# Two-batch head loads, value product before the maxima, and the first head's maxima beside the last query norm in a one-core decoder trunk

## The chip, the cores and the metric

The kernel runs on one core of a Trainium2 chip. The metric is the device time of one launch in microseconds. TensorE (PE) multiplies, ScalarE (ACT) and VectorE (DVE) work on its results, GpSimd (POOL) fills constants, SyncE (SP) issues nearly all DMAs; each engine runs its own instructions strictly in order and waits on semaphores for the others.

## The reference

One step of a two-layer decoder trunk over a prompt of 1,024 tokens with 16 meta tokens in front (1,040 rows) and a decode batch of 8 sequences of 4 tokens: layer 0 is a gated short convolution and an MLP, then one shared K/V/log-forget side is computed, layer 1 is forget-gated attention and an MLP. What matters here is the prompt's attention:

```
def forget_attention(q, k, v, c_q, c_k, q_pos, k_pos):
    s = einsum('nqhd,nkhd->nhqk', q, k) * HEAD_DIM ** -0.5
    s = s + (c_q[..., :, None] - c_k[..., None, :])     # c = cumsum of log f
    s = where(k_pos <= q_pos, s, -1e30)
    p = softmax(s, axis=-1)
    return einsum('nhqk,nkhd->nqhd', p, v)
```

There are 16 heads of 64 dimensions. q and k are RMS-normed per head. All is float32.

## The kernel before, in words

Float32 accuracy comes from splitting each operand into a rounded part (hi, float32r) and a rest (lo); a product is hi x hi + lo x hi + hi x lo. The rounding runs on ACT, the subtraction on DVE.

**Projections.** Weights come in units of 128 columns; `unit` (L415) multiplies one, 72 matmuls. The query units U_Q..U_Q+7 end the projection phase. For each, DVE scales the result into `KW` (L1667), ACT squares it, PE sums the squares per head (`column_sums`, L469), ACT takes the root, DVE finishes the norm into `QS` (`head_fin`, L1805), ACT and DVE split it into `STH`/`STL` (`stage_hi` L1548, `stage_lo` L1812) and SP stores both to DRAM (`stage_out`, L1361 and L1363). Keys were staged so before.

**Head operands.** `load_head(h)` fetches from DRAM what head h needs, into one of two halves (even and odd heads): six transfers of 260 KB (L929: `QA` = q hi, `CK` = k hi, `QB` = q lo and q hi, `DK` = k hi and k lo), the two rows of cumulated forget values (L930), and a zero row (L931), all on one semaphore. The tile names in the trace are q_hi_ext (QA), k_hi_ext (CK), q_lo_hi (QB), k_hi_lo (DK). SP's order in step h is: `spread_sums(h-1)` (L939), `load_inverse(h-1)` (L946, L949: store 1/sums, wait, fetch it broadcast), `load_v` at even h (L918, L919), `load_head(h+2)` once all logits of head h are done, `load_logf`.

**Maxima.** A head's row maxima come before its logits. `max_logits(h, u)` has 18 uses: 15 write hi x hi logits (L578, mask L581) to one of two PSUM banks in turn (4 and 5), DVE reduces each (L596); three ("A", "B", "C", L572) turn the maxima into a row that ACT copies into QA (`keep_shift`, L617). A use waits until the one two before it has been read. The maxima need QA and CK alone; QB and DK are first read by `logits`.

**The loop.** A head has 8 groups. PE's step t does `logits(t+2)` (L635, L636, L639), the maxima of head h+1 listed for this group, `weigh_values(t)` (L712 to L714). ACT takes two exponentials of each group (L658, L663), DVE the difference (`probs_lo`, L675), and then reduces the step's maxima; in group 4 it inverts the sums of head h-1 (L731) and in group 7 divides (L738). `max_logits(h+2, 0)` stands in step 8(h+1) and waits for the whole of `load_head(h+2)`.

**The start.** `attention_loads` loads head 0 after the stores of query block 6 (stage 14), `attention_vector` clears the value tiles on DVE, and POOL makes the mask (L1030) and, when stages 14 and 15 are stored, clears the odd half's tiles (`extend(1)`, from L1015) and `NMR` (L1038). The odd half's QA and CK lie where STH0/STL0 (even stages) were, QB and DK where STH1/STL1 were. DVE and PE start the maxima of head 0 after these.

## Time and profile before

| what | us |
|---|---|
| three runs, median (lowest to highest) | 3050.04 (3049.43 to 3050.2) |
| the profiled execution, its own time | 3054.29 |
| its span, first to last instruction | 3052.5 |
| PE busy | 2814.7 (92%) |
| DVE busy | 1189.4 (39%) |
| ACT busy | 792.0 (26%) |
| mean granted TensorE clock | 0.959 |

The shares are of the whole span. The prompt's attention takes about 1540 to 2017 us of it; in that stretch PE is busy in 6 to 8 tenths, elsewhere in 9. The profile's chain of work that ended last gives PE 85% and DMAs 4% of the span.

### The profile page before, as it was taken

How to read it: one execution, taken by the hardware profiler on the slowest of the kernel's cores; microseconds unless marked ns; L12 is line 12 of the kernel's file. 1: busy time of each engine (PE TensorE's matmuls, PEld its weight loads, DVE VectorE, ACT ScalarE, POOL GpSimd, SP SyncE). 2: the span in 40 equal slices, each digit the busy share in tenths (PEclk: the TensorE clock that was granted, in tenths of full speed). 3: DMA queues.
4: the chain of work that ended last, by engine and by line, in shares of the span. 5: the costliest groups of instructions: out<-in, count | busy, mean ns of one | idle time of the engine just before them, and what ended most of it. 6: DMA issues, size and time to landing. Idle time of an engine off the chain costs nothing.

```text
span 3052.5 us, 41584 instructions
## 1 busy us (share of the span) xinstructions
PE 2814.7 (92%) x17026; PEld 2729.9 (89%) x17026; DVE 1189.4 (39%) x1343; ACT 792.0 (26%) x1127; POOL 96.6 (3%) x65
## 2 busy tenths in 40 slices
PE   6999999999999999999967677767899999999999
PEld 5999999999999999999957666655799999999999
DVE  4444344133242333343455455554335223142331
ACT  4111121011110123532544444444322111011111
POOL 3000010000000002000000000000020000000000
PEclk8999999999999999999978888879899999999999
DMA  3111111111111111442343332323011111111112
GB/s 94 50 41 48 42 42 48 42 49 42 42 47 41 49 42 35 141 127 74 104 127 75 91 80 66 82 82 130 22 41 42 49 42 49 41 48 41 43 48 71
DMA packets 256005, 188.52 MB, mean 62 GB/s; under 512 B 15088, under 2 KB 237232, under 8 KB 255906
## 3 DMA queue, kind: packets, MB, share of 16 engines
q1 hardware_dynamic: 236802, 178.14, 20.6%
q10 hardware_dynamic: 19104, 8.99, 1.0%
q8 instruction: 71, 1.16, 0.2%
q14 instruction: 28, 0.23, 0.0%
HBM read 156.47 MB, written 30.49 MB: 61 GB/s over the span
## 4 chain that ended last, share of the span: by engine, by line
PE 85%; DMA 4%; DVE 3%; ACT 2%; SPq 2%; issue 1%; POOL 1%; ACTq 0%; DVEq 0%; POOLq 0%
PE ps L415 74%; DMA q_hi_ext<-k_hi_ext 3%; PE ps L578 2%; SPq L929 2%; PE ps L875 1%; PE ps L798 1%; DVE max_parts L596 1%; PE ps L712 1%; PE ps L713 1%; PE ps L714 1%; POOL t L450 1%; PE ps L635 1%; PE ps L469 1%; PE ps L636 1%; DMA inv_rows<-inv_spread 0%
## 5 line engine op out<-in xcount | busy, mean ns | idle before, releaser
L400 DVE TENSOR_TENSOR w_lo<-w_raw,w_hi 128x1024 fp32r<-128x1024 f32 x192 | 235.1, 1224 | 1234.5 <-ACT w_hi L392 1234.5
L415 PE MATMUL ps<-x_hi,w_hi 128*128 128x358 f32 x2688 | 594.6, 329 | 16.9 <-DVE x_lo L443 16.7
L415 PE MATMUL ps<-x_hi,w_lo 128*128 128x358 f32 x2688 | 591.0, 328 | 0.0
L415 PE MATMUL ps<-x_lo,w_hi 128*128 128x358 f32 x2688 | 589.9, 328 | 0.0
L392 ACT ACTIVATE w_hi<-w_raw 128x1024 fp32r<-128x1024 f32 x192 | 203.4, 1060 | 1324.4 <-PE ps L415 1324.4
L415 PEld LDWEIGHTS ps<-x_hi,w_hi 128*128 128x128 f32 x2688 | 465.7, 190 | 20.7 <-DVE x_lo L443 10.4
L415 PEld LDWEIGHTS ps<-x_lo,w_hi 128*128 128x128 f32 x2688 | 467.4, 190 | 0.0
L415 PEld LDWEIGHTS ps<-x_hi,w_lo 128*128 128x128 f32 x2688 | 466.4, 190 | 0.0
L415 PE MATMUL ps<-hid_hi,w_hi 128*128 128x358 f32 x1920 | 423.4, 329 | 3.1 <-DVE hid_lo L1215 3.1
L415 PE MATMUL ps<-hid_hi,w_lo 128*128 128x358 f32 x1920 | 420.8, 327 | 0.0
L415 PE MATMUL ps<-hid_lo,w_hi 128*128 128x358 f32 x1920 | 420.0, 327 | 0.0
L415 PEld LDWEIGHTS ps<-hid_hi,w_hi 128*128 128x128 f32 x1920 | 332.7, 190 | 3.3 <-issue 3.3
L415 PEld LDWEIGHTS ps<-hid_hi,w_lo 128*128 128x128 f32 x1920 | 332.5, 189 | 0.0
L415 PEld LDWEIGHTS ps<-hid_lo,w_hi 128*128 128x128 f32 x1920 | 331.8, 189 | 0.0
L578 PE MATMUL ps<-k_hi_ext,q_hi_ext 128*128 128x512 f32 (+5 forms) x240 | 101.0, 442 | 127.2 <-DMA q_hi_ext<-k_hi_ext 99.8
L578 PEld LDWEIGHTS ps<-k_hi_ext,q_hi_ext 128*128 128x128 f32 (+1 forms) x240 | 48.0, 204 | 149.4 <-DMA q_hi_ext<-k_hi_ext 93.2
L1454 ACT ACTIVATE hid_hi<-t 128x1074 f32 (+1 forms) x72 | 79.4, 1102 | 291.1 <-DVE t L1757 260.2
L1671 DVE TENSOR_TENSOR hid_lo<-t,hid_hi 128x1074 f32 (+1 forms) x72 | 92.0, 1278 | 100.1 <-ACT hid_hi L1454 100.1
L596 DVE TENSOR_REDUCE max_parts<-ps 128x1 f32<-128x512 f32 (+5 forms) x176 | 96.4, 564 | 43.0 <-PE ps L578 25.0
L450 POOL TENSOR_TENSOR t<-t,t 128x1074 f32<-128x1074 f32 x25 | 70.3, 2811 | 1275.4 <-ACT t L434 1274.9
L1731 DVE TENSOR_TENSOR acc<-ps,acc 128x1074 f32 (+1 forms) x80 | 101.5, 1269 | 22.4 <-PE ps L415 22.4
L675 DVE TENSOR_TENSOR probs_lo<-probs_f,probs_hi 128x768 fp32r<-128x768 f32 (+3 forms) x128 | 97.6, 762 | 26.9 <-ACT probs_hi L663 25.5
(228 smaller groups left out, 2514.7 us busy)
## 6 DMA issues: line engine op xcount, KB each, us to landing
w_raw<-in_mlp_w SPq DMA_DIRECT2D x128, 512.0 KB, 3.8
w_raw<-in_conv_w_in SPq DMA_DIRECT2D x24, 512.0 KB, 3.6
w_raw<-in_w_kv SPq DMA_DIRECT2D x16, 512.0 KB, 4.7
k_page<-in_cache_k SPq DMA_DIRECT2D x16, 512.0 KB, 4.1
v_page<-in_cache_v SPq DMA_DIRECT2D x16, 512.0 KB, 3.8
kh_rows<-staged_hi SPq DMA_DIRECT2D x8, 520.0 KB, 2.6
kl_rows<-staged_lo SPq DMA_DIRECT2D x8, 520.0 KB, 3.1
qh_rows<-staged_hi SPq DMA_DIRECT2D x8, 520.0 KB, 2.6
```

The source lines that it names most:

```text
L392: act.activation(WH[:, s], RAW[:, s], ACT.Copy).then_inc(w_hi, 1)
L400: dve.tensor_tensor(WL[:, s], RAW[:, s], WH[:, s].bitcast(F32), ALU.subtract).then_inc(w_lo, 1)
L415: mm = pe.matmul(PS[:, G * s + g, 0:GW], w[:, s, k], x[:, k, g * GW:(g + 1) * GW], start=(k == 0 and n == 0), stop=(k == KC - 1 and n == 2))
L450: pool.tensor_tensor(T2[:, 0:T], T2[:, 0:T], squares(f, m), ALU.add).then_inc(x_ssq, 1)
L469: mm = pe.matmul(PS[:, b, 0:GW], weights[:, :], x[:, g * GW:(g + 1) * GW], start=not stop, stop=stop)
L578: mm = pe.matmul(PS[0:rows, bank, 0:b - a], QA[hh][:, P * i:P * i + rows], CK[hh][:, a:b], start=True, stop=not diagonal)
L596: dve.tensor_reduce(to, PS[0:rows, bank, 0:b - a], mybir.AxisListType.X, ALU.max).then_inc(red_done, 1)
L675: dve.tensor_tensor(PBL[:, t % HI_RING, 0:nb * w], PF[:, t % 2, 0:nb * w], PBH[:, t % HI_RING, 0:nb * w].bitcast(F32), ALU.subtract).then_ ...
L929: sp.dma_start(to.bitcast(F32), src[rows]).then_inc(h_loaded[hh], 16)
L1454: act.activation(HH[:, j], T1[:, :], ACT.Copy).then_inc(hid_hi, 1)
L1671: dve.tensor_tensor(HL[:, j], T1[:, :], HH[:, j].bitcast(F32), ALU.subtract).then_inc(hid_lo, 1)
L1731: dve.tensor_tensor(banks(ACC[:, m]), result(c), banks(ACC[:, m]), ALU.add).then_inc(unit_read, 1)
```

## The change

`load_head` keeps the four transfers that the maxima need (QA, CK, the forget rows, the zero row); the other four become `load_cross`, on a semaphore of its own (`x_loaded`), for which `logits` waits at a head's first group. In the loop SP issues `load_head(h+2)`, `load_v`, `load_cross(h+2)` in this order. PE's step t does `logits(t+2)`, `weigh_values(t)`, then the maxima. At the start, head 0 is loaded after stage 12 and ahead of the two w_o units; POOL makes the mask as soon as the last projection unit is done, ACT rounds it before stage 14's rounding; PE does uses 0 to 4 of head 0, then the norm sums of the last query block, then the rest; DVE does uses 0 to 7, `head_fin` of the last block and some clears, uses 8 to 10, `stage_lo` of the last block, and the rest; POOL does the larger clears; head 1 is loaded in two parts, after stages 14 and 15.

```diff
-        MASKF, _ = place("mask_f32", [P, P], offset=early[0])
+        MASKF, _ = place("mask_f32", [P, P], offset=prompt_end[0])
@@ -560,7 +561,7 @@
             _, hh = head(h)
             x, bank, _ = use_of(h, u)
             if u == 0:
-                pe.wait_ge(h_loaded[hh], 128 * (h // 2 + 1))
+                pe.wait_ge(h_loaded[hh], 64 * (h // 2 + 1))
             ring_wait(h, u)
             if isinstance(x, str):
                 if x == "A":
@@ -626,6 +627,8 @@
             if h == HEADS:
                 return
             _, hh = head(h)
+            if g == 0:
+                pe.wait_ge(x_loaded[hh], 64 * (h // 2 + 1))
             if g == 0 or CHUNK_OF[g] != CHUNK_OF[g - 1]:
                 pe.wait_ge(nm_kept, N_SH * h + CHUNK_OF[g] + 1)
@@ -924,11 +927,19 @@
                 own, other = halves(hh)
                 o, rows = other.start, slice(HD * h, HD * h + HD)
                 ge(sp, st_done, NG * (h - 1))
-                for to, src in ((QA[hh][own], qh_rows), (CK[hh][own], kh_rows), (QB[hh][own], ql_rows),
-                                (QB[hh][other], qh_rows), (DK[hh][own], kh_rows), (DK[hh][other], kl_rows)):
+                for to, src in ((QA[hh][own], qh_rows), (CK[hh][own], kh_rows)):
                     sp.dma_start(to.bitcast(F32), src[rows]).then_inc(h_loaded[hh], 16)
                 sp.dma_start(CK[hh][o + 1:o + 3].bitcast(F32), c_rows[h]).then_inc(h_loaded[hh], 16)
                 sp.dma_start(QA[hh][o:o + 1].bitcast(F32), CK[hh][o + 3:o + 4].bitcast(F32)).then_inc(h_loaded[hh], 16)
+
+            def load_cross(h):
+
+                _, hh = head(h)
+                own, other = halves(hh)
+                rows = slice(HD * h, HD * h + HD)
+                for to, src in ((QB[hh][own], ql_rows), (QB[hh][other], qh_rows),
+                                (DK[hh][own], kh_rows), (DK[hh][other], kl_rows)):
+                    sp.dma_start(to.bitcast(F32), src[rows]).then_inc(x_loaded[hh], 16)
             def spread_sums(h):
@@ -950,17 +961,23 @@
             sp.wait_ge(c_stored, 32)
             sp.wait_ge(ext_ready, 4)
+            sp.wait_ge(st_kept[0], 32 * (KC // 2 + 1))
             load_head(0)
-            stage_out(2 * KC - 1)
+            load_cross(0)
+            for c in range(2):
+                load_unit(a["w_o"][0], 0, P * c, U_O + c)
+                stage_out(2 * KC - 3 + c)
             sp.wait_ge(unit_done, U_O)
-            sp.wait_ge(z_fin, 2 * KC)
+            sp.wait_ge(unit_read, U_O)
             sp.wait_ge(kv_stored, 48 * 2 * KC)
-            sp.wait_ge(vo_ones, 9)
+            sp.wait_ge(v_zero, 1)
             load_v(0)
             sp.wait_ge(st_kept[0], 32 * KC)
+            sp.wait_ge(ext_ready, 8)
+            load_head(1)
+            stage_out(2 * KC - 1)
             sp.wait_ge(st_kept[1], 32 * KC)
-            sp.wait_ge(ext_ready, 9)
-            load_head(1)
+            load_cross(1)
             sp.wait_ge(ids_loaded, 16)
             def load_pages(cache, to, index, done):
@@ -983,10 +1000,12 @@
                 if h:
                     spread_sums(h - 1)
                     load_inverse(h - 1)
+                if h + 2 < HEADS:
+                    load_head(h + 2)
                 if h % 2 == 0 and h + 2 < HEADS:
                     load_v(h // 2 + 1)
                 if h + 2 < HEADS:
-                    load_head(h + 2)
+                    load_cross(h + 2)
                 load_logf(h)
                 if h in (2, 4):
                     load_k(0, h // 2 - 1)
@@ -1026,16 +1045,18 @@
             pool.wait_ge(x_ssq, 24)
             extend(0)
             pool.wait_ge(unit_done, U_O)
-            pool.wait_ge(z_fin, 2 * KC)
             pool.memset(MASKF[:, :], 0.0).then_inc(p_const, 1)
             pool.wait_ge(p_const, 1)
             pool.affine_select(out=MASKF[:, :], in_=MASKF[:, :], compare_op=ALU.is_ge, fill=MASKED, base=0,
                                pattern=[[-1, P]], channel_multiplier=1).then_inc(p_const, 1)
             pool.wait_ge(p_const, 2)
             pool.wait_ge(st_kept[0], 32 * KC)
-            pool.wait_ge(st_kept[1], 32 * KC)
             extend(1)
-            pool.memset(NMR[:, :, :].bitcast(F32), 0.0).then_inc(ext_ready, 1)
+            for hh in range(2):
+                _, other = halves(hh)
+                pool.memset(VL[:, hh, :, other].bitcast(F32), 0.0).then_inc(vo_ones, 1)
+                pool.memset(VH[:, hh, 0:NT - 1, other].bitcast(F32), 1.0).then_inc(vo_ones, 1)
+                pool.wait_ge(vo_ones, 2 * hh + 2)
@@ -1066,15 +1087,10 @@
                 mask_of(i)
         def attention_scalar():
-            act.wait_ge(unit_done, U_O)
-            act.wait_ge(z_fin, 2 * KC)
-            act.wait_ge(p_const, 2)
-            act.activation(MASK[:, :], MASKF[:, :], ACT.Copy).then_inc(p_round, 1)
-            act.activation(IDR[:, :], ident[:, :], ACT.Copy).then_inc(p_round, 1)
-            act.activation(NID[:, :], ident[:, :], ACT.Copy, scale=-1.0).then_inc(p_round, 1)
+            keep_shift(0, "A")
             values_hi(0)
-            for x in "ABC":
-                keep_shift(0, x)
+            keep_shift(0, "B")
+            keep_shift(0, "C")
             for t in range(NG * HEADS):
                 exp_logits(t)
@@ -1129,22 +1145,7 @@
             for m in range(KC):
                 act.activation(HH[:, m], QS[:, m], ACT.Copy).then_inc(o_hi, 1)
-        def attention_vector():
-            dve.wait_ge(unit_done, U_O)
-            dve.wait_ge(z_fin, 2 * KC)
-            dve.memset(VRAW[:, NT - 1], 0.0).then_inc(vo_ones, 1)
-            for hh in range(2):
...
-            dve.memset(P8H[:, :, :].bitcast(F32), 0.0).then_inc(vo_ones, 1)
-            dve.memset(P8L[:, :, :].bitcast(F32), 0.0).then_inc(vo_ones, 1)
-            dve.wait_ge(vo_ones, 9)
-            for hh in range(2):
-                _, other = halves(hh)
-                dve.memset(VH[0:LASTP, hh, NT - 1, other].bitcast(F32), 1.0).then_inc(vo_ones, 1)
-            dve.wait_ge(ext_ready, 9)
+        def attention_vector(head_fin, stage_lo):
             def max_turn(h, u):
@@ -1155,8 +1156,26 @@
                         if n == REDS_FOR[x]:
                             join_max(h, x)
+            dve.wait_ge(unit_done, U_O)
+            dve.memset(VRAW[:, NT - 1], 0.0).then_inc(v_zero, 1)
+            dve.memset(NMR[:, :, :].bitcast(F32), 0.0).then_inc(v_zero, 1)
+            dve.wait_ge(v_zero, 2)
             for u in range(NUSE):
                 max_turn(0, u)
+                if u == 7:
+                    head_fin(2 * KC - 1, 1, G_QN, QS[:, KC - 1])
+                    for hh in range(2):
+                        _, other = halves(hh)
+                        dve.memset(VH[:, hh, NT - 1, other].bitcast(F32), 0.0).then_inc(v_zero, 1)
+                    dve.memset(P8H[:, :, :].bitcast(F32), 0.0).then_inc(v_zero, 1)
+                    dve.memset(P8L[:, :, :].bitcast(F32), 0.0).then_inc(v_zero, 1)
+                    dve.wait_ge(v_zero, 6)
+                    for hh in range(2):
+                        _, other = halves(hh)
+                        dve.memset(VH[0:LASTP, hh, NT - 1, other].bitcast(F32), 1.0).then_inc(v_zero, 1)
+                if u == 10:
+                    stage_lo(2 * KC - 1, QS[:, KC - 1, 0:NPR])
+            dve.wait_ge(vo_ones, 4)
             values_lo(0)
             probs_lo(0)
             for t in range(NG * HEADS):
@@ -1214,20 +1233,25 @@
                 dve.wait_ge(o_hi, m + 1)
                 dve.tensor_tensor(HL[:, m], QS[:, m], HH[:, m].bitcast(F32), ALU.subtract).then_inc(o_lo, 1)
-        def attention_tensor():
+        def attention_tensor(norm_sums):
             pe.wait_ge(p_round, 3)
-            pe.wait_ge(vo_ones, 11)
+            pe.wait_ge(unit_read, U_O)
             for u in range(NUSE):
                 max_logits(0, u)
+                if u == 4:
+                    for f in norm_sums.values():
+                        f()
             logits(0)
             logits(1)
+            pe.wait_ge(aux_read, AX_Q + 3 * KC)
+            pe.wait_ge(v_zero, 8)
             for t in range(NG * HEADS):
                 h, g = divmod(t, NG)
                 logits(t + 2)
+                weigh_values(t)
                 if h + 1 < HEADS:
                     for u in USE_AT[g]:
                         max_logits(h + 1, u)
-                weigh_values(t)
@@ -1389,9 +1413,6 @@
                 load_unit(a["w_q"][0], 0, P * n, U_Q + n)
                 if n >= 3:
                     stage_out(KC + n - 3)
-            for c in range(2):
-                load_unit(a["w_o"][0], 0, P * c, U_O + c)
-                stage_out(2 * KC - 3 + c)
             attention_loads(stage_out)
             with sp.Fori(1, KC // 2) as i:
                 for c in range(2):
@@ -1631,6 +1652,11 @@
             round_unit(U_Q + 2)
             for n in range(KC):
                 head_squares(U_Q, n)
+                if n == KC - 1:
+                    act.wait_ge(p_const, 2)
+                    act.activation(MASK[:, :], MASKF[:, :], ACT.Copy).then_inc(p_round, 1)
+                    act.activation(IDR[:, :], ident[:, :], ACT.Copy).then_inc(p_round, 1)
+                    act.activation(NID[:, :], ident[:, :], ACT.Copy, scale=-1.0).then_inc(p_round, 1)
                 if n:
                     stage_hi(KC + n - 1, QS[:, n - 1, 0:NPR])
                     round_unit(U_Q + n + 2)
@@ -1890,10 +1916,7 @@
                 if n:
                     stage_lo(KC + n - 1, QS[:, n - 1, 0:NPR])
                     cut_unit(U_Q + n + 2)
-            head_fin(2 * KC - 1, 1, G_QN, QS[:, KC - 1])
-            stage_lo(2 * KC - 1, QS[:, KC - 1, 0:NPR])
-
-            attention_vector()
+            attention_vector(head_fin, stage_lo)
             residual_turns(U_O, 4)
@@ -2036,10 +2059,7 @@
             with pe.Fori(1, KC // 2) as i:
                 unit(U_Q, i, mid=head_sums(U_Q, 1, ax(AX_Q - 3, 6, i), KC + 2 * i - 1))
                 unit(U_Q + 1, i, mid=head_sums(U_Q, 0, ax(AX_Q, 6, i), KC + 2 * i))
-            for f in head_sums(U_Q, 1, ax(AX_Q + 3 * (KC - 1), 0, 0), 2 * KC - 1).values():
-                f()
-
-            attention_tensor()
+            attention_tensor(head_sums(U_Q, 1, ax(AX_Q + 3 * (KC - 1), 0, 0), 2 * KC - 1))
             eight(U_O, 0, HH, HL, o_ready)
             mlp(1, 4, 3)
```

## Rows read from the trace of the kernel before

**Rows 1.** PE's waits, 1595 to 2005 us: total us, times, longest
```profile
PE ps L578 <- DMA q_hi_ext<-k_hi_ext: 90.3, 14, 9.0
PE ps L578 <- DVE max_parts L596: 12.1, 14, 0.9
```
**Rows 2.** Stretches: us, busy us (instructions) of PE, PEld, DVE, ACT, POOL, PEclk, DMA share, GB/s
```profile
1602.00:1976.50 374.50, 270.36 (x1716) 247.46 (x1716) 204.42 (x377) 166.57 (x325) 0.00 (x0) 0.86 0.35 81
...
1619.00:1623.00 4.00, 4.00 (x35) 3.91 (x33) 2.12 (x6) 2.40 (x6) 0.00 (x0) 1.00 0.83 206
1623.00:1628.00 5.00, 1.07 (x7) 0.87 (x7) 2.16 (x3) 2.63 (x5) 0.00 (x0) 0.97 1.00 212
1743.90:1747.70 3.80, 0.00 (x0) 0.00 (x0) 0.00 (x0) 0.00 (x0) 0.00 (x0) 0.50 0.62 130
1747.70:1754.00 6.30, 6.27 (x24) 6.03 (x25) 2.34 (x5) 1.90 (x4) 0.00 (x0) 0.50 0.00 0
1754.00:1770.00 16.00, 14.65 (x108) 13.29 (x107) 11.63 (x24) 8.98 (x20) 0.00 (x0) 1.00 0.17 44
```
**Rows 3.** Timeline, head loads of 1602 to 1630: start, us, engine, line, [idle <- releaser]
```profile
1602.11 0.47 PE L578 MATMUL ps<-k_hi_ext,q_hi_ext 128*128 128x128 f32 x1 [3.79 <-DMA q_hi_ext<-k_hi_ext]
1616.84 0.24 DVE L731 RECIPROCAL inv_spread<-sums_spread 65x16 f32<-65x16 f32 x1
1618.44 0.51 SPq L949 DMA_DIRECT2D inv_sums<-inv_rows  x1
1619.00 0.59 SPq L929 DMA_DIRECT2D q_hi_ext<-qh_rows  x1
1623.31 0.55 SPq L931 DMA_DIRECT2D q_hi_ext<-k_hi_ext  x1
1629.21 0.48 PE L578 MATMUL ps<-k_hi_ext,q_hi_ext 128*128 128x128 f32 x1 [5.14 <-DMA q_hi_ext<-k_hi_ext]
```
**Rows 4.** Timeline of one head's cycle, 1736 to 1764
```profile
1736.61 0.50 SPq L949 DMA_DIRECT2D inv_sums<-inv_rows  x1
1740.17 1.23 DVE L738 TENSOR_TENSOR q_all<-o_and_sums,inv_sums 64x1040 f32<-64x1040 f32 x1 [0.74 <-DMA inv_sums<-inv_rows]
1747.73 0.48 PE L578 MATMUL ps<-k_hi_ext,q_hi_ext 128*128 128x128 f32 x1 [7.38 <-DMA q_hi_ext<-k_hi_ext]
1749.40 0.63 PE L712 MATMUL ps<-probs_hi,v_hi 128*128 128x384 f32 x1
1751.64 0.52 PE L635 MATMUL ps<-q_hi_ext,k_hi_ext 128*128 128x256 f32 x1
1763.00 0.25 DVE L731 RECIPROCAL inv_spread<-sums_spread 65x16 f32<-65x16 f32 x1
```
**Rows 5.** Timeline, PE at full clock: one value product between two logits groups
```profile
1993.54 0.28 PE L712 MATMUL ps<-probs_hi,v_hi 128*128 128x272 f32 x1
1994.29 0.34 PE L635 MATMUL ps<-q_hi_ext,k_hi_ext 128*128 128x384 f32 x1
```
**Rows 6.** Timeline of the first head's start, 1537 to 1573
```profile
1540.87 1.05 ACT L1548 ACTIVATE staged_hi<-q_all 128x1040 fp32r<-128x1040 f32 x1
1542.40 0.67 PE L469 MATMUL ps<-squares_r,ones_per_head 128*128 128x358 f32 x1 [5.13 <-DVE squares_r L1799]
1543.41 1.22 DVE L400 TENSOR_TENSOR w_lo<-w_raw,w_hi 128x1024 fp32r<-128x1024 f32 x1
1546.75 1.34 DVE L1805 SCALAR_TENSOR_TENSOR q_all<-k_work,vectors,t 128x1074 f32<-128x1074 f32 x1 [2.12 <-ACT t L1557]
1554.48 0.44 PE L578 MATMUL ps<-k_hi_ext,q_hi_ext 128*128 128x128 f32 x1 [9.49 <-DMA q_hi_ext<-k_hi_ext]
1556.57 0.96 POOL L1015 MEMSET k_hi_ext<- 64x1040 f32 x1 [7.69 <-DMA ql_rows<-staged_lo]
1561.13 0.69 PE L578 MATMUL ps<-k_hi_ext,q_hi_ext 128*128 128x384 f32 x1 [5.56 <-DVE row_max L596]
1572.66 0.67 PE L635 MATMUL ps<-q_hi_ext,k_hi_ext 128*128 128x384 f32 x1
```

More of the change, by code:

```diff
@@ L327, in trunk @@
         p_const, p_round, ext_ready = sem("p_const"), sem("p_round"), sem("ext_ready")
-        h_loaded, sm_loaded, inv_stored, inv_loaded = (
-            [sem(f"{x}{i}") for i in range(2)] for x in ("h_loaded", "sm_loaded", "inv_stored", "inv_loaded"))
+        h_loaded, x_loaded, sm_loaded, inv_stored, inv_loaded = (
+            [sem(f"{x}{i}") for i in range(2)]
+            for x in ("h_loaded", "x_loaded", "sm_loaded", "inv_stored", "inv_loaded"))
         v_loaded, v_hi, v_lo = sem("v_loaded"), sem("v_hi"), sem("v_lo")
@@ L333, in trunk @@
         pv_done, acc_free = sem("pv_done"), sem("acc_free")
-        vo_ones, inv_done, o_fin = sem("vo_ones"), sem("inv_done"), sem("o_fin")
+        v_zero, vo_ones, inv_done, o_fin = sem("v_zero"), sem("vo_ones"), sem("inv_done"), sem("o_fin")
         ids_loaded, lp_loaded, vn_loaded = sem("ids_loaded"), sem("lp_loaded"), sem("vn_loaded")
@@ L1130, in attention_scalar @@
                 act.activation(HH[:, m], QS[:, m], ACT.Copy).then_inc(o_hi, 1)
-        def attention_vector():
-            dve.wait_ge(unit_done, U_O)
-            dve.wait_ge(z_fin, 2 * KC)
-            dve.memset(VRAW[:, NT - 1], 0.0).then_inc(vo_ones, 1)
-            for hh in range(2):
-                _, other = halves(hh)
-                dve.memset(VH[:, hh, 0:NT - 1, other].bitcast(F32), 1.0).then_inc(vo_ones, 1)
-                dve.memset(VH[:, hh, NT - 1].bitcast(F32), 0.0).then_inc(vo_ones, 1)
-                dve.memset(VL[:, hh, :, other].bitcast(F32), 0.0).then_inc(vo_ones, 1)
-            dve.memset(P8H[:, :, :].bitcast(F32), 0.0).then_inc(vo_ones, 1)
-            dve.memset(P8L[:, :, :].bitcast(F32), 0.0).then_inc(vo_ones, 1)
-            dve.wait_ge(vo_ones, 9)
-            for hh in range(2):
-                _, other = halves(hh)
-                dve.memset(VH[0:LASTP, hh, NT - 1, other].bitcast(F32), 1.0).then_inc(vo_ones, 1)
-            dve.wait_ge(ext_ready, 9)
+        def attention_vector(head_fin, stage_lo):
             def max_turn(h, u):
```

## The prediction

> **What bounds the kernel now.** I read the page's busy tenths first: PE is busy nine tenths nearly everywhere and only six to eight in the attention, where the granted clock is lower too, so that stretch is where time can be won. Then PE's waits: in 410 us of attention PE waits 14 times, 90.3 us in all, for the last small transfer of a head's operands, and only 12.1 us for DVE's reductions [rows 1]. Then the stretches [rows 2]: from one head's first maximum at 1602 to that of the 13th head after it at 1976.5, 374.5 us, a head takes 28.8 us. PE is busy 20.8 us of it (270.36/13), DVE 15.7, ACT 12.8. PE's 8.0 idle microseconds are 6.5 for the operands and 1.5 of short waits. Last, the clock: after a wait of 7.38 us [rows 4] PE works 6.3 us at 0.50, then at 1.00 [rows 2]; the clock was at 0.50 from 1743.9 on, some 3.5 us after PE had stopped at 1740.35. A mean clock of 0.86 is 0.14 x 2 x 28.8 = 8.1 us at half clock in each head; about 6.5 - 3.5 = 3.0 of them are idle, the other 5.1 hold work that would take half as long. So a head is 18.2 us of work at full clock, 2.6 extra for the half clock, 6.5 operand wait, 1.5 short waits.
>
> Why does the load come so late? A cycle runs through DMA and PE: reciprocal of the last head's sums on DVE, store and refetch of them on SP, eight load issues, landing, PE's first maximum, and PE and DVE on to the next reciprocal. From the reciprocal to the first maximum it is 12.4 us (1616.84 to 1629.21 [rows 3]). The eight issues take seven steps of 0.62 us, and from 1619 to 1628 the DMA engines are full at some 210 GB/s [rows 2]: the 1.8 MB (6 x 260 KB, and 260 KB of inverses ahead of them) are bound by bandwidth.
>
> **The change, part by part. 1. Two batches.** The first issue stays 2.2 us after the reciprocal. The fourth, now the zero row, comes three steps later, at 4.0 instead of 6.5 us. Inverses, QA and CK are 0.8 MB, which had moved by 1623.0 (4 us at 206 GB/s [rows 2]), 6.2 us after the reciprocal. Data ended about 1628.0 and PE went on at 1629.2, so landing takes 1.3 more: 7.5 us. That needs the later batch not to delay the earlier. A row speaks for it: the inverses, issued at 1736.61 with six large transfers right behind, released DVE's division at 1740.17, 3.6 us later [rows 4], while the queue stayed full to beyond 1743.9 [rows 2]. Bounds: 6.2 us (data through, no landing time) and 12.4 us (as now); between them, with the zero row as long under way as now, 5.9 us from its issue, it is 9.9. I take 7.5, nearest to the inverses' row.
>
> At even heads `load_v` moves behind the first batch. It no longer adds its 0.5 MB and two issues before the maxima; instead it lands some 2.5 us behind them (0.53 MB at 210 GB/s), and ACT, which rounds the values behind a copy that needs PE's product, waits there up to 2 us. PE's next need of a new exponential lies a group and a half (some 5 us) later, so I count nothing; without that cover it would be 2 us in 7 heads, 14 us. The second batch lands when the eighth transfer does now, about 12.4 us (15 with the values) after the reciprocal. PE needs it at the head's first logits, six steps after its first maximum, at about 20 us. Nothing waits; its four issues stay ahead of the forget page and the next `spread_sums`, whose result is wanted a head later.
>
> **2. Value product ahead of the maxima.** No instruction is added. The product of group 0 takes 2.24 us at half clock (1749.40 to 1751.64 [rows 4]), 1.1 at full, and now runs before the wait instead of after it. PE stood at the wait 7.2 us after the reciprocal (1629.21 - 5.14 - 1616.84 [rows 3]). A product of group 4 (0.75 us at full clock [rows 5]) moves ahead of the reciprocal in exchange. And DVE has time for a reduction while PE multiplies: of 1.5 us of short waits I take 0.5 as gone. PE now arrives at 7.2 + 1.1 - 0.75 - 0.5 = 7.1, and waits 0.4. What is added is that the product stands directly behind `logits(t+2)` and needs DVE's difference of its group. That difference has been at the head of DVE's queue for most of a step, so I price it at 0; its bounds are a gain of the whole 1.5 and a loss of one difference per step (0.55 to 0.96 us long, some 6 us a head).
>
> **3. The new cycle.** From first maximum to next reciprocal it was 15.3 us (1747.73 to 1763.00 [rows 4]). Off come 2.24 (product of group 0, now before) and half of the 4.1 us left at half clock, 2.0; 0.75 is added: 11.8. With 7.5 that is 19.3 us. PE by itself: 28.8 - 6.5 - 2.6 = 19.7 with its old short waits, 19.2 with 0.5 of them gone. Both limits coincide, and DVE is busy 15.7 us of it, in order, with its heaviest two steps (5.1 us) where PE has 3.6. So what is saved in one place is partly waited out in another: I take 20.0, 0.7 above the cycle. Waits of well under 3.5 us leave the clock up: the 16 us from 1754 with 1.35 us of PE idle in them are at 1.00 throughout [rows 2]. Gain 8.8 us x 13 = 114 us.
>
> **4. Ends of the chain.** From head 0's first logits to head 2's first maximum it was 29.45 us (1572.66 [rows 6] to 1602.11 [rows 3]): the wait of 3.79 goes, 1.1 of product comes ahead: -2.5 with rounding. After head 15's first maximum (1976.5) no load follows, but the stretch no longer starts cold with 6.3 us, nor with that product: 3.1 + 1.1 = -4.
>
> **5. The first head.** Now PE waits 9.49 us for head 0's load, then 5.56 for DVE, which stands behind POOL's clears, which stand behind the store of stage 15; head 0's first logits are at 1572.66 [rows 6]. Afterwards the load has landed long before (it needs stage 12 alone). The mask is made once the last projection unit is done (1537.3, which is 1542.40 - 5.13). ACT's three roundings, 0.6 us, come before its stage 14 rounding, at 1540.9, so PE does uses 0 and 1 at 1541.6. DVE, pushed by these 0.6 us, ends its weight cut (1543.41 + 1.22 [rows 6]) at about 1545.1; with two small clears use 2 follows at 1545.8. From use 2 to the first logits took 11.5 us (1561.13 to 1572.66 [rows 6]). Put into it are the norm sums on PE, 2.6 (from 1542.40), `head_fin` 1.3, the clears left on DVE 0.9, `stage_lo` 1.2, none with much to hide it because uses alternate between PE and DVE: 17.5, logits at 1563.3. Gain 9.4, between 3 (each insert doubled by hand-overs) and 15 (inserts hidden). POOL's and SP's work for head 1 is done by about 1553 (QA, CK) and 1568 (rest); it is needed at about 1567 and past 1580.
>
> **Sum.** 114 + 2.5 + 4 + 9.4 = 130 us off the profiled execution's 3054.3 gives 2924.3. The median of the runs is 4.3 lower than that execution: 2920. Range of this case alone: 2900 to 2940.
>
> **Rivals.** *A, the small row is the limit:* its 5.9 us stay. Cycle 9.9 + 11.8 = 21.7, 1.7 more in 14 heads: 2944. For it: that row is last in both orders and one transfer may sit behind a slow engine. Against it: in rows 3 the bytes ahead explain all of the 5.9. *B, the batches land together:* 12.4 + 11.8 = 24.2, waits of some 5 us cool the clock again: (4.2 + 2.6) x 14 = 95, 3015. Against it is the inverses' row. *C, more than I count:* all short waits go, PE alone sets 18.2 + 0.1: 1.7 x 14 less, 2896. DVE's 15.7 us in order speak against. *D, slower:* shorter but more frequent waits of PE on the two PSUM banks hold the clock at 0.50. Then 18.2 us of work become 36.4, 38 with waits, 18 more than 20.0 in 13 periods: 3154. It decides when 8.8 of the 18.2 us are at half clock, for that eats the gain. Against it are the 16 us at 1.00 with such waits, and that the change makes idle time smaller [rows 2].
>
> The Trainium skill has the rule behind D (TensorE: Matmul & The Clock Gate, "A second HAM failure mode: psum-queue depth-cycling"): small idles between groups of matmuls that cycle through PSUM banks made the clock swing in one kernel. By that rule this change would not give the 2.6 us back and could lose more; the trace does not agree so far, with 1.00 over those 16 us.
>
> **Chances.** Forecast 0.66, A 0.16, B 0.04, C 0.10, D 0.04. The predicted time is 2920. The range takes in A and C and some of the unpriced waits: 2890 to 2958. A measurement tells 0.2% (6 us) from no change. Forecast, A, B and C are all faster; adding something for an unforeseen stall: faster 0.94, same 0.02, slower 0.04.
>
> **What would show it.** Step 1: from a reciprocal to the next head's first maximum 7 to 8 us instead of 12.4; PE's wait for the zero row under 1 us, or about 2.5 if A. Step 2: short waits of a head at about 1 us, none on DVE's difference at the value products. Step 3: a head in 20 us, clock 1.00 from about 1580 to 1980; a clock of 0.50 there would be D. Step 4 and 5: first logits of head 0 near 1563. The forecast is wrong if a head takes over 22 us, and then the releaser ahead of PE's idle tells whether DMA, DVE or ACT took the operands' place.

## The result, and the profile after

The median is 2932.61 us (2931.66 to 2934.36, four runs) against 3050.12 (3049.43 to 3050.54): ratio 0.9616, interval [0.9599, 0.9632], 117.5 us off. The profiled execution took 2932.93 where that of before took 3054.29: 121.4 less. Forecast were 130.

The page's head and busy line of the changed kernel:

```profile
span 2931.1 us, 41586 instructions
PE 2783.4 (95%) x17026; PEld 2701.3 (92%) x17026; DVE 1186.8 (40%) x1340; ACT 786.3 (27%) x1127; POOL 98.2 (3%) x68
```

PE's busy time fell by 31 us although it does the same instructions, for fewer of them ran at half clock (the mean granted clock is 0.979 for 0.959); the other 90 us were idle time. PE's waits in the attention, 1590 to 1880 us (total us, times, longest):

```profile
PE ps L579 <- DVE max_parts L597: 11.3, 14, 1.1
PE ps L579 <- DMA q_hi_ext<-k_hi_ext: 8.9, 12, 1.6
PE ps L579 <- ACT q_hi_ext L618: 5.4, 14, 0.4
PE ps L579 <- DVE row_max L597: 1.7, 11, 0.2
```

The wait for the operands, 90.3 us [rows 1], is 8.9; that for DVE's reductions (`max_parts`) is about what it was. No wait for DVE's difference at the value product is in the list. Stretches (columns as in [rows 2]): 13 heads, from first maximum to first maximum, then one head, then 3.3 us behind a wait of 1.44 us:

```profile
1586.00:1855.50 269.50, 241.32 (x1718) 221.56 (x1717) 204.82 (x378) 162.84 (x329) 0.00 (x0) 0.99 0.49 113
...
1652.30:1672.40 20.10, 18.32 (x132) 16.82 (x132) 15.55 (x30) 12.02 (x25) 0.00 (x0) 1.00 0.43 91
...
1608.70:1612.00 3.30, 3.30 (x15) 3.30 (x14) 1.42 (x2) 0.87 (x2) 0.00 (x0) 0.55 0.28 54
```

374.5 us [rows 2] became 269.5. One load, timeline (start, us, engine, line, [idle <- releaser]), against [rows 3]:

```profile
1643.92 0.25 DVE L734 RECIPROCAL inv_spread<-sums_spread 65x16 f32<-65x16 f32 x1
1644.20 0.36 SPq L957 DMA_DIRECT2D inv_rows<-inv_spread  x1
...
1645.54 0.49 SPq L960 DMA_DIRECT2D inv_sums<-inv_rows  x1
1646.08 0.59 SPq L931 DMA_DIRECT2D q_hi_ext<-qh_rows  x1
1646.72 1.05 SPq L931 DMA_DIRECT2D k_hi_ext<-kh_rows  x1
1647.82 0.44 SPq L932 DMA_DIRECT2D k_hi_ext<-c_rows  x1
1648.30 0.56 SPq L933 DMA_DIRECT2D q_hi_ext<-k_hi_ext  x1
1648.90 0.59 SPq L942 DMA_DIRECT2D q_lo_hi<-ql_rows  x1
...
1652.27 0.33 PE L579 MATMUL ps<-k_hi_ext,q_hi_ext 128*128 128x128 f32 x1 [0.67 <-DMA q_hi_ext<-k_hi_ext]
...
1664.36 0.25 DVE L734 RECIPROCAL inv_spread<-sums_spread 65x16 f32<-65x16 f32 x1
```

From the reciprocal to the first maximum it is 8.35 us instead of 12.4, and PE stands still for 0.67 of them instead of 5.14. (The 12.4 were among the shortest before: over the 13 heads it was 12.3 to 16.2 us, 14.0 on average, and 14.4 to 16.2 at the six heads that have the value load ahead of the operands.) The next reciprocal comes 12.1 us later. The slowest load of the trace:

```profile
1620.98 0.24 DVE L734 RECIPROCAL inv_spread<-sums_spread 65x16 f32<-65x16 f32 x1
...
1624.86 0.56 SPq L933 DMA_DIRECT2D q_hi_ext<-k_hi_ext  x1
1625.46 1.21 SPq L921 DMA_DIRECT2D v_raw<-out_v_prompt  x1
...
1630.29 0.33 PE L579 MATMUL ps<-k_hi_ext,q_hi_ext 128*128 128x128 f32 x1 [1.64 <-DMA q_hi_ext<-k_hi_ext]
```

Here the issue behind the zero row took 1.21 us where most take 0.6, and PE went on 5.4 us after the zero row's issue instead of 4.0: 9.31 us from the reciprocal. The first head's start, against [rows 6]:

```profile
1537.42 1.33 DVE L1831 SCALAR_TENSOR_TENSOR q_all<-k_work,vectors,t 128x1074 f32<-128x1074 f32 x1
1540.53 0.48 PE L579 MATMUL ps<-k_hi_ext,q_hi_ext 128*128 128x128 f32 x1 [4.34 <-ACT minus_ident L1659]
1544.40 0.69 PE L579 MATMUL ps<-k_hi_ext,q_hi_ext 128*128 128x384 f32 x1 [2.75 <-DVE row_max L597]
...
1553.78 0.69 PE L579 MATMUL ps<-k_hi_ext,q_hi_ext 128*128 128x384 f32 x1 [2.16 <-ACT q_hi_ext L618]
...
1560.21 0.66 PE L638 MATMUL ps<-q_hi_ext,k_hi_ext 128*128 128x384 f32 x1
```

Head 0's logits begin at 1560.21 instead of 1572.66. The 121.4 us are thus 105.0 in the 13 periods, 12.45 before head 0's logits, 3.65 from there to head 2's first maximum (25.80 for 29.45), and 0.4 after head 15's (1075.6 for 1076.0).

### The profile page after: what moved, and what is told of

Read it like the earlier page. It is cut to its first block, busy times and chain, and to the rows that moved or that the text cites. A ratio compares the mean times of both kernels' runs of the same rounds, so it can differ in the third digit from the quotient of the medians.

```text
span 2931.1 us, 41586 instructions
## 1 busy us (share of the span) xinstructions
PE 2783.4 (95%) x17026; PEld 2701.3 (92%) x17026; DVE 1186.8 (40%) x1340; ACT 786.3 (27%) x1127; POOL 98.2 (3%) x68
## 4 chain that ended last, share of the span: by engine, by line
PE 88%; DVE 3%; DMA 3%; ACT 2%; issue 1%; POOL 1%; SPq 1%; ACTq 0%; DVEq 0%; POOLq 0%
PE ps L416 77%; DMA q_hi_ext<-k_hi_ext 2%; PE ps L878 1%; PE ps L801 1%; PE ps L579 1%; DVE max_parts L597 1%; POOL t L451 1%; PE ps L638 1%; PE ps L715 1%; PE ps L716 1%; PE ps L717 1%; PE ps L470 1%; PE ps L639 1%; DVE probs_lo L678 1%; PE ps L502 0%
## 5 line engine op out<-in xcount | busy, mean ns | idle before, releaser
L416 PE MATMUL ps<-x_hi,w_hi 128*128 128x358 f32 x2688 | 593.8, 329 | 18.5 <-DVE x_lo L444 18.4
L416 PEld LDWEIGHTS ps<-x_hi,w_hi 128*128 128x128 f32 x2688 | 465.4, 191 | 22.1 <-DVE x_lo L444 11.8
L579 PE MATMUL ps<-k_hi_ext,q_hi_ext 128*128 128x512 f32 (+5 forms) x240 | 89.5, 397 | 41.4 <-DVE max_parts L597 12.8
L597 DVE TENSOR_REDUCE max_parts<-ps 128x1 f32<-128x512 f32 (+5 forms) x176 | 96.2, 563 | 39.0 <-PE ps L582 21.1
L579 PEld LDWEIGHTS ps<-k_hi_ext,q_hi_ext 128*128 128x128 f32 (+1 forms) x240 | 41.8, 178 | 62.0 <-DVE max_parts L597 23.6
```

What stands on the lines that cost most here:

```text
L416: mm = pe.matmul(PS[:, G * s + g, 0:GW], w[:, s, k], x[:, k, g * GW:(g + 1) * GW], start=(k == 0 and n == 0), stop=(k == KC - 1 and n == 2))
L579: mm = pe.matmul(PS[0:rows, bank, 0:b - a], QA[hh][:, P * i:P * i + rows], CK[hh][:, a:b], start=True, stop=not diagonal)
L597: dve.tensor_reduce(to, PS[0:rows, bank, 0:b - a], mybir.AxisListType.X, ALU.max).then_inc(red_done, 1)
```

## The experiments

Each was compared with the kernel before on the same chip, where that one took 3052.4 to 3053.2 us; the numbers to go by are the ratios. e1 to e4 ran on one chip, e5 to e8 on a second, e9 and e10 on a third. Line numbers of an experiment can differ by a few from those above.

**e1: the two batches alone**, in the kernel before:

```diff
-                pe.wait_ge(h_loaded[hh], 128 * (h // 2 + 1))
+                pe.wait_ge(h_loaded[hh], 64 * (h // 2 + 1))
...
+                if h + 2 < HEADS:
+                    load_head(h + 2)
                 if h % 2 == 0 and h + 2 < HEADS:
                     load_v(h // 2 + 1)
                 if h + 2 < HEADS:
-                    load_head(h + 2)
+                    load_cross(h + 2)
```

> The kernel before with the two load batches alone; maxima stay ahead of the value product, the first head starts as before. Theory (the gain is the load path, and a head's cycle runs reciprocal, load, first maximum, next reciprocal): the first maximum comes 8.1 us after the reciprocal as in the changed kernel (12.4 before), the stretch from first maximum to reciprocal is 12.2 us at full clock, so a head takes 20.3 to 20.8 us and the time is 2945 to 2955 (before minus about 13 x 8 us). Rival (the product ahead of the wait is what covers the rest of the load): the wait stays at 2 us or more in every head, the clock falls after it each time, a head takes 22 us or more and the time is 2970 to 2985.

2951.58 us, ratio 0.9673 [0.9656, 0.9691]. Timeline, one head:

```profile
1652.07 0.25 DVE L734 RECIPROCAL inv_spread<-sums_spread 65x16 f32<-65x16 f32 x1
...
1661.35 0.33 PE L579 MATMUL ps<-k_hi_ext,q_hi_ext 128*128 128x128 f32 x1 [2.00 <-DMA q_hi_ext<-k_hi_ext]
...
1675.52 0.25 DVE L734 RECIPROCAL inv_spread<-sums_spread 65x16 f32<-65x16 f32 x1
```

The first maximum comes 7.8 to 9.3 us after the reciprocal with the old order on PE as well, and the time lies in the theory's range. The last eight of the 13 heads, without half clock, took 20.4 to 20.8 us; behind two longer waits for operands the clock fell, and the heads took 22.9 and 23.0. This one edit is worth some 100 us of the 117.5.

**e2: the order alone**, in the kernel before:

```diff
                 logits(t + 2)
+                weigh_values(t)
                 if h + 1 < HEADS:
                     for u in USE_AT[g]:
                         max_logits(h + 1, u)
-                weigh_values(t)
```

> The kernel before with the value product ahead of the next maxima, nothing else. Theory: the load path of 12.4 us (more at even heads) sets the cycle and PE waits long whatever stands before the wait; only the product of group 0 moves out (2.2 us at half clock) and one of group 4 in (0.75), the rest of the cold start gets longer, so 0.3 to 1.3 us a head: 3030 to 3046. Rival (short waits of PE on DVE's reductions were a large share, or waits on DVE's difference appear): 3015 and less, or 3055 and more.

3048.78 us, ratio 0.9992 [0.9983, 1.0002]: not to be told from no change, and just above the theory's range. Timeline, one even head:

```profile
1701.04 0.25 DVE L731 RECIPROCAL inv_spread<-sums_spread 65x16 f32<-65x16 f32 x1
...
1708.62 0.56 SPq L931 DMA_DIRECT2D q_hi_ext<-k_hi_ext  x1
...
1715.55 0.48 PE L578 MATMUL ps<-k_hi_ext,q_hi_ext 128*128 128x128 f32 x1 [6.82 <-DMA q_hi_ext<-k_hi_ext]
```

From reciprocal to first maximum it is 12.3 to 15.5 us here: the load sets the cycle. The product ahead of it shortens the idle time and hardly the cycle (28.4 us a head over the twelve periods from head 3 to head 15, where it was 28.9).

**e3: both, with the start of the kernel before.** Its `attention_vector`, `attention_scalar` and `attention_tensor` begin as before, the norm sums ahead of them (shown against the changed kernel, a part of it):

```diff
             for u in range(NUSE):
                 max_logits(0, u)
-                if u == 4:
-                    for f in norm_sums.values():
-                        f()
...
+            for f in head_sums(U_Q, 1, ax(AX_Q + 3 * (KC - 1), 0, 0), 2 * KC - 1).values():
+                f()
+
+            attention_tensor()
```

> Batches and order as in the changed kernel, but the first head's start of the kernel before. Theory: the start is worth what the two traces show between the last query norm and head 0's first logits, 11.4 us, so 2943 to 2946. Rival (part of it is given back because the later loads then meet, or the earlier start makes the slow heads 2 to 4): 2932 to 2938.

2940.60 us, ratio 0.9636 [0.962, 0.9652], between the two ranges. Against e1 the order is now worth 11 us, 0.8 a head, with some 7 us of uncertainty either way. The start is worth the rest to the changed kernel: 0.0020 of the time before (6 us) by its first ratio, 0.0032 (10 us) by the one it got beside the later experiments (e5, below). These intervals touch or overlap; e10 measures the start by itself.

**e4: the first batch of a head issued in the gap between store and refetch of the inverses**, in the changed kernel:

```diff
                 sp.dma_start(inv_rows[h].rearrange("(p x) -> p x", x=16), SI[:, hh]).then_inc(inv_stored[hh], 16)
+                if between:
+                    between()
                 sp.wait_ge(inv_stored[hh], 16 * (m + 1))
...
-                    load_inverse(h - 1)
-                if h + 2 < HEADS:
+                    load_inverse(h - 1, (lambda: load_head(h + 2)) if h + 2 < HEADS else None)
+                elif h + 2 < HEADS:
```

> The changed kernel, with the first batch of head h+2 issued between the store and the refetch of the inverses, in the 1.3 us in which SyncE waits for the store. Theory: the first issue comes 0.8 instead of 2.2 us after the reciprocal and no longer behind the inverses' 260 KB, so the operands land 5.5 to 6 us after it, before PE stands at the wait (7.1 us); PE and DVE then set the cycle at 19.2 to 19.6 us instead of 20.7 on average, no head falls to half clock: 2908 to 2918. Rival (DVE in order is already the limit, or the later inverses hold DVE's division and with it the differences): a head stays at 20 us or takes longer, and the time is 2928 or more.

2938.49 us, ratio 0.9628 [0.9612, 0.9644]: the rival. DVE's wait ahead of the division and PE's ahead of its third maxima, 1590 to 1880:

```profile
DVE q_all L741 <- DMA inv_sums<-inv_rows: 20.1, 13, 2.5
...
PE ps L579 <- DVE row_max L597: 18.4, 13, 2.4
```

PE's wait for operands is gone, but the inverses, now behind the batch, make DVE's division wait up to 2.5 us. The reductions for the maxima stand behind it in DVE's order, and PE waits for them instead. The theory also had no head at half clock; in this trace it fell three times, during or behind waits of 1.95 to 2.15 us for those reductions.

**e5: the changed kernel once more, unedited,** to see whether its slow loads recur.

> The changed kernel once more, unaltered, beside the next ones and for a second profile. In its first profile three loads (heads 3, 4, 15) landed 9.1 to 9.3 us after the reciprocal instead of 8.1, in each SyncE's fifth issue took 1.2 to 1.5 us instead of 0.6, and PE then worked 3.4 us at half clock. Theory (these are chance, a hiccup of the queue, not the program's order): the slow heads fall elsewhere, and the times spread over 2930 to 2936. Rival (they come from the start, which puts head 2's load on top of head 1's): heads 3 and 4 are slow again.

2929.96 us, ratio 0.9604 [0.9588, 0.962]. PE's wait for the operands in the same stretch:

```profile
PE ps L579 <- DMA q_hi_ext<-k_hi_ext: 6.7, 13, 1.0
```

None over 1.0 us, and no half clock. Heads 3 to 5 took 20.7, 20.4 and 20.5 us for 21.4, 22.9 and 22.0, and the 13 periods were 264.2 us, 20.3 each. But neither the theory nor the rival holds as written, for the slow issues stand at the same heads again. In e5 it is another transfer of the same load that is issued slowly, at head 3 and at head 15:

```profile
1601.94 1.48 SPq L931 DMA_DIRECT2D k_hi_ext<-kh_rows  x1
...
1847.59 1.49 SPq L942 DMA_DIRECT2D q_lo_hi<-qh_rows  x1
```

Among the operand and value loads of heads 3 to 15, issues over 1.0 us stand at heads 3, 4, 5 and 15 and nowhere else in both traces of the changed kernel, and so in e3, e4, e6 and e8 (e1 has them at 3, 4, 6 and 7). At head 14 the inverses are refetched 2.5 us after the reciprocal instead of 1.6, in both traces again. So heads 3 to 5, 14 and 15 are the late ones (8.3 to 8.9 us from reciprocal to first maximum in e5, 7.8 to 8.3 in the others). What changes from run to run is which transfer is hit: where it was the one behind the zero row (heads 3, 4 and 15 in the first trace) PE went on after 9.1 to 9.3 us, and half clock followed. Why these heads, no run shows.

**e6: the values' load ahead of the first batch again:**

```diff
-                if h + 2 < HEADS:
-                    load_head(h + 2)
                 if h % 2 == 0 and h + 2 < HEADS:
                     load_v(h // 2 + 1)
                 if h + 2 < HEADS:
+                    load_head(h + 2)
+                if h + 2 < HEADS:
                     load_cross(h + 2)
```

> The changed kernel, with the value transfer ahead of the first batch again (0.5 MB and two issues, at even heads only). Theory: the first batch of even heads lands 2.2 to 2.5 us later, 10.3 to 10.6 us after the reciprocal; PE waits 2.5 to 3 us there; since waits of 1.4 to 1.6 us were already followed by half clock, each of these 7 heads loses 2.3 us and 1.5 us more: 27 us, 2957 to 2963. Rival (half clock needs a wait as long as the 3.5 us before it fell in the kernel before): 7 x 2.3 = 16 us, 2946 to 2951.

2953.79 us, ratio 0.9679 [0.9663, 0.9695], between the two ranges; that half clock followed shorter waits than 3.5 us is the theory's side. Timeline of an even head and the stretch behind its wait:

```profile
1619.57 0.24 DVE L734 RECIPROCAL inv_spread<-sums_spread 65x16 f32<-65x16 f32 x1
...
1630.40 0.47 PE L579 MATMUL ps<-k_hi_ext,q_hi_ext 128*128 128x128 f32 x1 [3.19 <-DMA q_hi_ext<-k_hi_ext]
```

```profile
1632.90:1636.20 3.30, 3.30 (x13) 3.20 (x13) 0.88 (x2) 0.87 (x2) 0.00 (x0) 0.50 0.80 289
```

At the even heads from 4 to 14 the first maximum comes 10.1 to 11.9 us after the reciprocal, 2.0 to 3.0 later than in e5, PE waits 2.4 to 3.8 us, and half clock comes during the wait or behind it. Head 2, the seventh with a value load, has no such wait. So in six heads this costs 23 us (0.9679 against 0.9604): moving 0.53 MB behind the first batch is a quarter of what the batches bring. What is issued ahead of a transfer delays it. What is issued behind it hardly does, as far as the value load shows: in the changed kernel heads 6, 8, 10 and 12, which have its 0.53 MB directly behind the first batch, took 8.00 us on average from reciprocal to first maximum, heads 7, 9, 11 and 13, which have not, 8.06. No run leaves the second batch out.

**e7: e4, and the division of head h-1 moved from step 7 to the next head's step 0:**

```diff
-                if h and g == 7:
-                    divide(h - 1)
+                if h > 1 and g == 0:
+                    divide(h - 2)
+            divide(HEADS - 2)
```

> e4 (first batch issued between store and refetch of the inverses) and in addition the division of a head two groups later in VectorE's order, behind the maxima of the next head's first group. In e4 PE no longer waited for operands, but DVE's division waited 20.1 us in 13 heads for inverses that now land later, and PE 18.8 us for the maxima behind it. Theory (that was the only thing that took the gain): both waits go, a head takes 19.2 to 19.7 us: 2912 to 2922. Rival (DVE's 15.7 us of work in order set 20 us whatever it waits for, or ACT now waits for the division before it copies a head's first chunk): 2930 or more.

2922.30 us, ratio 0.9576 [0.956, 0.9592]: the fastest version, 0.3 us above the theory's range. Its 260 us from 1600, and two rows of its timeline:

```profile
1600.00:1860.00 260.00, 237.03 (x1713) 217.96 (x1714) 200.18 (x377) 159.60 (x325) 0.00 (x0) 1.00 0.51 116
```

```profile
1638.85 0.25 DVE L734 RECIPROCAL inv_spread<-sums_spread 65x16 f32<-65x16 f32 x1
...
1646.36 0.28 PE L579 MATMUL ps<-k_hi_ext,q_hi_ext 128*128 128x128 f32 x1
```

PE comes to the first maximum 7.5 us after the reciprocal and finds its operands there; a head takes 20.0 to 20.1 us, at full clock throughout. The two waits on transfers are gone, yet the head does not come down to the theory's 19.2 to 19.7: this much of the rival holds. What remains is PE's 18.2 busy us and short waits for the reductions and the shift row; those for `row_max` are 6.1 us in 13 heads where the changed kernel had 1.7, and DVE now waits 32.4 us for ACT's exponentials where it waited 7.7.

**e8: the division moved, without e4.** The same edit of the division as in e7, in the changed kernel.

> The changed kernel with that later division alone. Theory (a head's cycle runs through the load; the division lies beside PE's wait for it): 1.2 us of DVE move from before the wait to behind it, no gain, 2930 to 2942. Rival (DVE's order is what keeps a head at 20 us): 0.5 to 1 us a head faster, 2918 to 2926.

2931.02 us, ratio 0.9605 [0.9589, 0.9621]: no gain by itself, against e5's 0.9604. So in e7 it is the early load that won (0.9576 against 0.9605, 9 us, intervals that just overlap), once the division no longer stood in its way.

**e9: e7 with the order on PE of the kernel before:**

```diff
                 logits(t + 2)
-                weigh_values(t)
                 if h + 1 < HEADS:
                     for u in USE_AT[g]:
                         max_logits(h + 1, u)
+                weigh_values(t)
```

> The kernel with the first operands fetched between values and divide, but with the next head's first maximum matmuls ahead of the value product again, as in the kernel before. Theory: the value product's place in front was worth its cover for the wait on the first operands; where those have landed before TensorE is free, the order is worth only short waits of at most 0.4 us a head, so 2922 to 2928, with no wait of TensorE on the transfer of q_hi_ext or k_hi_ext over 1 us. Rival: the order is worth as much here as it was with the two batches alone (about 12 us or more), 2933 or above.

2927.90 us, ratio 0.9585 [0.9569, 0.9601]. No wait for operands, clock 1.00 throughout, a head in 20.25 us: 0.2 us a head more than e7. PE's waits for the row maxima in 1590 to 1880, e9 and e7:

```profile
PE ps L579 <- DVE row_max L597: 8.5, 13, 0.7
```

```profile
PE ps L579 <- DVE row_max L597: 6.1, 13, 0.5
```

So of the 0.8 us a head that the order brought in e3, some 0.2 is left where there is no wait on operands. The rest was cover for that wait, but not all of it is the wait's own length: in heads 8 to 14, at full clock in both, a head took 20.6 us in e1 and 20.1 in e3, and what the order brought beyond these 0.5 fell to the early heads, two of which ran at half clock in e1 and none in e3. The medians of e7 and e9 differ by 5.6 us, but their intervals overlap, so it is the traces that tell them apart.

**e10: the new start alone.** The changed kernel with one load order and the old order on PE:

```diff
-                if h + 2 < HEADS:
-                    load_head(h + 2)
                 if h % 2 == 0 and h + 2 < HEADS:
                     load_v(h // 2 + 1)
                 if h + 2 < HEADS:
+                    ...
+                        sp.dma_start(to.bitcast(F32), src[rows]).then_inc(h_loaded[h % 2], 16)
                     load_cross(h + 2)
+                    ...
```

> The kernel before with only the new start: head 0's maxima beside the last query norm; one order of the load and the old order on TensorE everywhere else. Theory: the start is worth about 11 us by itself, as nothing later takes it back: 3039 to 3043, with head 0's first logit matmul 11 to 12 us earlier than before. Rival: part of it is given back, at most 6 us stay, because head 1 and 2 wait for their operands instead: 3046 or above, though the first logit matmul is as early.

3039.88 us, ratio 0.9958 [0.9944, 0.9972], 13 us off: the theory. PE's waits, 1580 to 1995 us, and head 0's first logits:

```profile
PE ps L579 <- DMA q_hi_ext<-k_hi_ext: 90.3, 14, 8.6
```

```profile
1560.31 0.66 PE L638 MATMUL ps<-q_hi_ext,k_hi_ext 128*128 128x384 f32 x1
```

The logits begin 12.35 us earlier, of which 0.6 is there already at the query norm ahead of it (1537.92 against 1538.51); the 14 waits of the later heads come to the same 90.3 us as before, so nothing is given back.

## Why the prediction was right, step by step

Predicted were 2920 us and a range of 2890 to 2958; the time is 2932.61. It lies inside that range and inside the case's own 2900 to 2940. The mechanism held and no rival took over. The median is 12.6 us above the forecast: 8.6 of them are the sum's (121.4 for 130), mis-sized in the heads by 9, at the ends by 2.5 and at the start by -3 us; the other 4 are that I took the median to lie 4.3 below the profiled execution, as before, and it lies 0.3 below.

**Step 1, batches.** Predicted 7.5 us from reciprocal to first maximum. In the eight periods that ran undisturbed it was 7.8 to 8.4, 8.0 on average, in the five others 8.35 to 9.3. The step's premise, that the batch behind does not delay the one in front, is borne out: 8.0 us with the second batch behind it in every head, and no later where the value load stands behind it too. Rival B (together, 12.4) is refuted by every head; rival A (9.9) was met by none, PE going on 4.0 us after the zero row's issue, 5.4 in the slowest. The gain was sized by the whole head, 28.8 us, and not by the 12.4 of one head, which was below the average of 14.0; so that reading did no harm. The value load behind the batch makes ACT wait 8.1 us in all (six times, longest 3.0), and no wait of PE behind it shows in the trace: priced at 0, right.

**Step 2, order.** PE arrived 7.7 us after the reciprocal (1652.27 - 0.67 - 1643.92) for 7.1 predicted, and waited 0.67 for 0.4. Short waits came to 18.4 us in 14 heads, 1.3 each where I had 1.0: of the 0.5 us that DVE was to gain, 0.2 came. The price of 0 for standing behind DVE's difference is right.

**Step 3, the cycle.** Predicted 20.0 us a head and 114 in 13. The eight undisturbed heads took 20.1 on average (19.9 to 20.5), 12.1 from first maximum to reciprocal for 11.8 predicted: right within 0.1. The way there is partly luck. The load path was 0.5 longer and the rest 0.3 longer than priced, 20.1 together and not 19.3, which is about as much as the 0.7 that I had added for something else, for work waited out. The 0.7 has its own ground all the same: with the load out of the way (e7) PE and DVE keep a head at 20.0 to 20.1, where I had 19.2 for them. The other five took 21.1 to 22.9, 8.2 us more than five times 20.1. That is the 9 us of the step. It contains what was wrong in it: "waits of well under 3.5 us leave the clock up". After waits of 1.44, 1.64 and 1.54 us the clock was at 0.50 for some 3.4 us, which put 3.1 us into the two periods behind the first two (13.63 us from first maximum to reciprocal for 12.08); the other 5.1 us are the later landings themselves. In e5, with no wait over 1.0, the 13 periods were 5.3 us shorter. The forecast had no term for loads that come up to a microsecond late at certain heads (3 to 5, 14 and 15, in both traces), nor for their double price. The trace of before has such irregular issues as well, 1.35 and 1.50 us in the loads of heads 4 and 6.

**Step 4, ends.** From head 0's logits to head 2's first maximum it was -3.65 us for -2.5. Behind head 15's first maximum -0.4 for -4: the last of the three waits falls there and the stretch begins at half clock after all (stretch 1857.7 to 1860.6). In e5 the same stretch was 2.7 shorter than before. So of the 4 us the first trace shows 0.4 and the second 2.7.

**Step 5, start.** Predicted -9.4, measured -12.45, of which 1.1 lies ahead of the attention (the query norm at 1537.42 for 1538.51), so -11.4 belong to the step. First maxima 1540.5 for 1541.6, use 2 at 1544.4 for 1545.8, and from there to the first logits 15.8 us for 17.5: the inserts were partly hidden. e10 shows -13 us by itself (-17 to -9 by its interval); against e3 the changed kernel shows -6 by its first ratio and -10 by e5's.

**The sum.** By the ratios of e1, e3 and e5: batches 0.0327, the order with them 0.0037, the start with both 0.0032 of the time before, 100, 11 and 10 us (with the changed kernel's first ratio the last is 6). The batches are beyond doubt; the other two are known to within some 7 us each. Rival C (all short waits go, 2896) needed DVE not to matter; even e7, with no wait for operands, keeps 1.6 us a head of short waits for ACT's and DVE's results (22.8 us in 14) and stays at 20.0. Rival D (the clock stays at 0.50, 3154) was wrong here: the trace shows 1.00 over whole heads with waits of 0.4 to 1.1 us in each, and over 260 us in e7. The Trainium skill's rule behind it (TensorE: Matmul & The Clock Gate, "A second HAM failure mode: psum-queue depth-cycling") was not borne out in the prompt's attention by any run. Behind it, in the decode batch's attention, which this change leaves alone, the granted clock does swing, as the last section shows; whether from the page's cause, no run here tries.

## What to carry to other kernels

When a consumer waits for the last of several transfers, ask which of them its first step needs and give those a semaphore of their own and the front of the queue; here that one edit made 100 of 117.5 us, and a bulk load of 0.53 MB left in front of them would have cost a quarter of it. Price a transfer's wait with its spread, not its median, look whether the late transfers stand at the same places in a second trace before calling them chance, and count the clock that a wait takes along. A reordering on the waiting engine is worth little while the load sets the cycle (e2), something as cover (e3), and little again when the load is early (e9), so fix the load first; and before moving a transfer forward, look for who needs what it passes (e4), since it may be one more move that turns the loss into the gain (e7).

## What the runs showed of the hardware that was not expected

The clock. In the prompt's attention of these traces, from head 2 on, no wait of PE up to 1.0 us was followed by half clock (0.50), and with every one from 2.5 us on it came, during the wait or behind it. Between them the length does not decide. Half clock came with waits of 1.44, 1.64 and 1.54 us in the changed kernel, 2.00 and 1.48 in e1, 1.14 in e3, and 2.15, 1.95 and 2.14 in e4; it did not come with 1.14 in the changed kernel, 1.70, 1.38 and another 1.48 in e1, 1.34 in e3, nor even 2.41 in e4. It can begin as late as 2.3 us after PE has gone on (e6). What decides is open.

Behind the prompt's attention the clock does swing, in the kernel before as well. In the decode batch's attention of the changed kernel a turn takes some 17 us, PE waits 1.0 and then 1.8 to 2.0 us in it, and behind the longer wait it works 3.4 us at half clock, in six turns in a row from 1946 to 2035 us:

```profile
1945.14 0.32 PE L801 MATMUL ps<-k_t_hi,q_blocks_hi 128*64 128x288 f32 x1 [1.84 <-issue]
...
1946.30:1949.50 3.20, 3.20 (x15) 2.98 (x14) 0.00 (x0) 0.00 (x0) 0.00 (x0) 0.50 0.53 154
```

An issue of SP that mostly takes 0.6 us took 1.05 to 1.7 us in some loads; in six of the traces (both of the changed kernel, e3, e4, e6 and e8) these were the loads of heads 3, 4, 5 and 15. In the changed kernel and e3, PE went on 1.0 to 1.3 us late, against the 8.0 of most heads, where the slow issue was the one behind the zero row; but in e1 head 5 came after 9.28 us with no issue over 1.0. The cause was not tried.
